# First norm, modulation rows and condition rows of a two-block fp32 layer, rearranged over the engines

## The reference

```
mx = (silu(c) @ ada_w + ada_b).reshape(6, 1024)        # 48 groups of 128 columns: j = 0..47
mc = (silu(c_ctx) @ ada_w + ada_b).reshape(6, 1024)    # only its first two rows are read
hx = x   * rsqrt(mean(x*x)   + EPS) * norm1_g * (1 + mx[1]) + mx[0]
hc = ctx * rsqrt(mean(ctx*ctx) + EPS) * norm1_g * (1 + mc[1]) + mc[0]
ux, uc = hx @ w_in, hc @ w_in
# gates f = lb + (1-lb)*sigmoid(u_f) ; k = 1-f ; q = silu(u_q) ; bidirectional scan over the tokens
# mx[2] scales the mixer's residual, mx[3], mx[4] modulate the second norm, mx[5] the FFN's residual
```

## Time and profile before

| what | value |
|---|---|
| median of 3 runs | 951.21 us (949.1 to 951.27) |
| the profiled execution's own time | 950.52 us |
| its span in the trace | 948.3 us |
| TensorE matmuls busy | 874.2 us (92%) |
| VectorE busy | 588.7 us (62%) |
| ScalarE busy | 463.9 us (49%) |
| GpSimd busy | 409.7 us (43%) |
| mean granted clock of TensorE | 0.965 |

### The profile page before, as it was taken

How to read it: one execution, slowest core, us unless ns; L and a number is a source line. 1 busy time by engine, 2 the same in 40 slices (tenths; PEclk the granted TensorE clock), 3 DMA queues, 4 the chain that set the end, 5 groups by cost and what they waited for, 6 DMA issues and landing times. The chain is left out here.

```text
span 948.3 us, 16413 instructions
## 1 busy us (share of the span) xinstructions
PE 874.2 (92%) x6668; PEld 832.1 (88%) x6668; DVE 588.7 (62%) x1218; ACT 463.9 (49%) x755; POOL 409.7 (43%) x180
## 2 busy tenths in 40 slices
PE   3599978999997899999999989999999999999995
PEld 0268968999976899999999989989999999999995
DVE  4888856555457878777667567977545543333335
ACT  3363223333274566555555576445444565455543
POOL 3455412221010028888888710000000788888881
PEclk9779997999999899999999999999999999999997
DMA  9677653443156645656665544625444455566641
GB/s 354 248 246 255 234 200 113 132 134 101 54 184 216 184 152 175 207 181 182 191 180 179 179 143 138 197 67 177 135 134 134 154 180 184 177 185 189 182 152 46
DMA packets 46043, 162.53 MB, mean 171 GB/s; under 512 B 5248, under 2 KB 5392, under 8 KB 45840
## 3 DMA queue, kind: packets, MB, share of 16 engines
q1 hardware_dynamic: 45680, 160.43, 52.6%
q10 hardware_dynamic: 288, 1.05, 0.4%
HBM read 160.41 MB, written 1.05 MB: 170 GB/s over the span
## 5 line engine op out<-in xcount | busy, mean ns | idle before, releaser
L476 POOL TENSOR_TENSOR wlo<-raw,whi 128x1024 fp32r<-128x1024 f32 x160 | 387.5, 2441 | 461.8 <-ACT whi L1069 461.7
L1069 ACT ACTIVATE whi<-raw 128x1024 fp32r<-128x1024 f32 (+1 forms) x253 | 258.1, 1026 | 85.6 <-PE bank L604 44.5
L604 PE MATMUL bank<-h2l,whi 128*128 128x256 f32 x848 | 240.4, 284 | 2.5 <-DVE h2l L1459 2.4
L600 PE MATMUL bank<-h2h,whi 128*128 128x256 f32 x848 | 241.6, 285 | 0.5 <-ACT h2h L1286 0.5
L602 PE MATMUL bank<-h2h,wlo 128*128 128x256 f32 x848 | 239.9, 283 | 0.0
L1459 DVE SCALAR_TENSOR_TENSOR accs<-bank,vec,accs 128x189 f32<-128x189 f32 (+4 forms) x440 | 161.2, 433 | 72.2 <-ACT accs L1331 72.2
L604 PEld LDWEIGHTS bank<-h2l,whi 128*128 128x128 f32 x848 | 162.7, 192 | 3.5 <-DVE h2l L1459 3.5
L600 PEld LDWEIGHTS bank<-h2h,whi 128*128 128x128 f32 x848 | 162.7, 192 | 1.4 <-ACT h2h L1286 0.7
L602 PEld LDWEIGHTS bank<-h2h,wlo 128*128 128x128 f32 x848 | 162.7, 192 | 0.1
L476 DVE TENSOR_TENSOR wlo<-raw,whi 128x1024 fp32r<-128x1024 f32 (+1 forms) x93 | 104.5, 1131 | 40.6 <-ACT whi L1069 40.2
L886 PE MATMUL bank<-gl,whi 128*128 128x256 f32 x352 | 99.7, 283 | 1.3 <-DVE gl L1456 1.3
(11 more groups left out here) (303 smaller groups left out, 1673.5 us busy)
## 6 DMA issues: line engine op xcount, KB each, us to landing
raw<-in_up SPq DMA_DIRECT2D x88, 512.0 KB, 3.6
raw<-in_w_in SPq DMA_DIRECT2D x45, 512.0 KB, 3.7
raw<-in_down SPq DMA_DIRECT2D x44, 512.0 KB, 3.9
ada_buf<-in_adaT SPq DMA_DIRECT2D x40, 512.0 KB, 4.3
raw<-in_w_out SPq DMA_DIRECT2D x16, 512.0 KB, 3.6
raw<-in_w_in_t SPq DMA_DIRECT2D x12, 512.0 KB, 4.7
ada_sc<-in_ada SPq DMA_DIRECT2D x8, 512.0 KB, 14.0
raw<-in_wk SPq DMA_DIRECT2D x8, 512.0 KB, 3.8
```

The lines of the kernel that those rows point to most:

```text
L476: return e.tensor_tensor(wlo[:, j % HL, 0:k], raw[:, j % RAW, 0:k], whi[:, j % HL, 0:k].bitcast(F32), ALU.subtract)
L600: e.matmul(ps, wh[:, k, :], xh(k), start=k == 0, stop=False)
L604: t = e.matmul(ps, wh[:, k, :], xl(k), start=False, stop=k == KTILES[name] - 1)
L1069: e.activation(whi[:, j % HL, 0:(k1 - k0) * 128], raw[:, j % RAW, 0:(k1 - k0) * 128], ACT.Copy).then_inc(S.hi.up(j))
```

## The change

Seven things are changed, all before the end of the scan:

- The condition rows come as two DMAs of 4 KB into one partition (`crow`), get one silu, and TensorE spreads them over 128 partitions into four PSUM banks (`row_of`). The 16 sums of groups 0 to 7 read them there. ScalarE copies the x row to `cb` in an SBUF place that lasts, so that the later reload and silu are gone.
- The squares go into 8 tiles of their own (`sqs`), and TensorE sums all of them, 32 small matmuls into one bank, ahead of the scale rows. GpSimd's additions are gone.
- The norm's row is copied to SBUF (`rsx`), and GpSimd multiplies x and context with it (`xr`). VectorE then needs one `tensor_scalar` (times amul, plus shift) for each half tile, written to a PSUM bank; ScalarE's addition of the shift is gone.
- `amul` is made ahead of the last pair of sums, and columns 0 and 1 are made side by side by `lins`.
- The loads are put in another order: a short first part of `vec` and all of x and context first, the convolution's vectors later, the chunks 16 to 18 before the wait for the first low halves.
- The groups 16 to 47 go round three buffers of their own (in the places of `kT` and `vM`, which are written later).
- Their sums stand elsewhere: one behind each ff column in place of two, none in front of `qx` in place of eight, and two in each of the eight calls of `beside`, which had none. The last eight stay where they were.

```diff
-ADA_OF = [[j] + ([j + 6] if j < 2 else []) + (list(range(12 + j, 48, 2)) if j > 3 else []) for j in range(6)]
+ADA_OF = [[j] + ([j + 6] if j < 2 else []) for j in range(6)] + [list(range(16 + j, 48, 3)) for j in range(3)]
...
+        put("sqs", 94 + 16, [128, 8, 512])
+        put("crow", 94, [1, 2, 1024])
+        put("xr", 94, [128, 8, 512])
+        put("rsx", 92, [128, 512])
+        put("ada_kT", 20, [128, 2, 1024])
+        put("cb", 28, [128, 1024])
+        put("ada_vM", 32, [128, 1024])
...
+        def ada_at(j):
+
+            s = next(s for s in range(9) if j in ADA_OF[s])
+            if s < 6:
+                return s, M["ada_buf"][:, s, :]
+            return s, M["ada_kT"][:, s - 6, :] if s < 8 else M["ada_vM"][:, :]
+
+        def ht_bank(k):
+            return aux_bank(("ht", k))
+
+        def row_of(who):
+
+            first = 4 if who else 2
+            return psum[:, first:first + 2, :].rearrange("p a b -> p (a b)")
...
+            one_row = cst[0:1, 1:2].broadcast_to((1, 128))
...
+            for who, ring, first in ((0, lin_ring, 0), (1, aux_ring, 4)):
+                w.wait_ge(S.const, "cst")
+                w.wait_ge(S.rowc, "crow")
+                for half in range(2):
+                    slot, _ = ring.take(("row", who, half), S.ada, 7)
+                    t = e.matmul(banks[first + slot], one_row, M["crow"][:, who, half * 512:half * 512 + 512], start=True,
+                                 stop=True)
+                t.then_inc(S.rows.up(("cb", "cbx")[who]))
+
+            slot, _ = aux_ring.take("x", S.by_row, "x")
+            w.wait_ge(S.const, "ones")
+            for i in range(8):
+                w.wait_ge(S.sqx, i)
+                for b in range(4):
+                    t = e.matmul(banks[4 + slot][:, b:b + 1], M["sqs"][:, i, b * 128:b * 128 + 128], ones[:, 0:1],
+                                 start=i == 0 and b == 0, stop=i == 7, skip_group_check=True)
+            t.then_inc(S.total.up("x"))
+            w.wait_ge(S.ident, 0)
+            spread("x", aux_bank("x"))
...
             for k in range(KT):
-                if k == 4:
-                    means("x", M["ssx"], 4, S.ssx, 7, (S.scaled, 7))
...
-            for j in range(8):
+            for k in range(KT):
+                ht_bank_free[k] = aux_ring.take(("ht", k), S.hcl, k)[1]
+
+            columns = []
+            for j in range(2):
+                slot, free = lin_ring.take(("ff", j), S.sgf, j)
+                columns.append(("w_in", IN_FF + j, banks[slot][:, :], free))
+            lins(columns, hc_all)
+            for j in range(2, 8):
...
+            w.wait_ge(S.crow, "ctx")
+            e.activation(crow[:, :, :], crow[:, :, :], ACT.Silu).then_inc(S.rowc.up("crow"))
...
-            w.wait_ge(S.cb, "first")
-            e.activation(cb[:, :], cb[:, :], ACT.Silu).then_inc(S.rowc.up("cb"))
-            w.wait_ge(S.cbx, 0)
-            e.activation(cbx[:, :], cbx[:, :], ACT.Silu).then_inc(S.rowc.up("cbx"))
+            w.wait_ge(S.rows, "cb")
+            e.activation(M["cb"][:, :], row_of(0), ACT.Copy).then_inc(S.rowc.up("cb"))
             for i in range(8):
                 w.wait_ge(S.x[i // 4], 0)
+                e.activation(M["sqs"][:, i, 0:L], xT[:, i, :], ACT.Square)
                 w.wait_ge(S.ctx[i // 4], 0)
-                out = M["ssx"]
-                if i:
-                    w.wait_ge(*sq_free["x", i])
-                    out = sq_at(("x", i))
-                e.activation(out[:, 0:L], xT[:, i, :], ACT.Square)
-                e.activation(out[:, L:2 * L], M["ctxT"][:, i, :], ACT.Square).then_inc(S.sqx.up(i))
+                e.activation(M["sqs"][:, i, L:2 * L], M["ctxT"][:, i, :], ACT.Square).then_inc(S.sqx.up(i))
             w.wait_ge(S.const, "cst")
             sqrt_next()
             w.wait_ge(S.total, "x")
             root("x", aux_bank("x")[:, 0:4])
+            by_row("x", M["rsx"][:, :], aux_bank("x"))
...
-            splits(HL)
-            w.wait_ge(S.mod, "shift")
+            splits(2)
             for k in range(KT):
-                ht = hs_at(k)
                 w.wait_ge(S.scaled, k)
-                for v in range(2):
-                    t = e.activation(ht[:, v * L:v * L + L], ht[:, v * L:v * L + L], ACT.Identity,
-                                     bias=M["mod"][:, k, v:v + 1])
-                t.then_inc(S.hch.up(("shift", k)))
-                w.wait_ge(S.hch, ("shift", k))
-                e.activation(M["hch"][:, k, :], ht, ACT.Copy).then_inc(S.hch.up(("hi", k)))
+                e.activation(M["hch"][:, k, :], ht_bank(k), ACT.Copy).then_inc(S.hch.up(k))
+                if k in (3, 6):
+                    splits(2 + k // 3)
...
             for j in range(KT):
-                w.wait_ge(S.rowc, "cbx")
+                w.wait_ge(S.rows, "cbx")
+                w.wait_ge(S.rowc, "cb")
                 if j:
                     w.wait_ge(own_dve, own_dve.n)
-                ada_sum(j, 1, junk[:, :], cbx[:, :]).then_inc(own())
+                ada_sum(j, 1, junk[:, :], row_of(1)).then_inc(own())
                 w.wait_ge(own_dve, own_dve.n)
-                ada_sum(j, 0, ada_buf[:, slot_of(j), :], cb[:, :]).then_inc(S.ada.up(j))
-                if j == 4:
+                ada_sum(j, 0, None, row_of(0)).then_inc(S.ada.up(j))
+                if j == 1:
                     inverse("x")
-            w.wait_ge(S.rows, "turned")
-            two = (128, 8, 2)
-            tt(mod[:, 8:16, :], aux_bank("turned")[:, 0:16].rearrange("p (j w) -> p j w", w=2),
-               col("ada_b", 8, 8).unsqueeze(2).broadcast_to(two), ALU.add).then_inc(S.mod.up("scale"))
-            w.wait_ge(S.mod, "scale")
-            stt(amul[:, :, :], mod[:, 8:16, :], 1.0, col("norm1_g", 0, 8).unsqueeze(2).broadcast_to(two), ALU.add,
-                ALU.mult).then_inc(S.mod.up("amul"))
+                if j == 6:
+                    w.wait_ge(S.rows, "turned")
+                    tt(mod[:, 8:16, :], aux_bank("turned")[:, 0:16].rearrange("p (j w) -> p j w", w=2),
+                       col("ada_b", 8, 8).unsqueeze(2).broadcast_to(two), ALU.add).then_inc(S.mod.up("scale"))
...
-            w.wait_ge(S.spread, "x")
-            w.wait_ge(S.mod, "amul")
-            for k in range(KT + 3):
+            w.wait_ge(S.mod, "shift")
+            for k in range(KT + 2):
                 if k < KT:
-                    if k >= 4:
-                        w.wait_ge(S.hcl, k - 4)
-                    for v, src in enumerate((xT, M["ctxT"])):
-                        t = stt(hs_at(k)[:, v * L:v * L + L], src[:, k, :], amul[:, k, v:v + 1],
-                                aux_bank("x")[:, v * L:v * L + L], ALU.mult, ALU.mult)
+                    w.wait_ge(*ht_bank_free[k])
+                    w.wait_ge(S.xr, k)
+                    for v in range(2):
+                        t = e.tensor_scalar(ht_bank(k)[:, v * L:v * L + L], M["xr"][:, k, v * L:v * L + L],
+                                            amul[:, k, v:v + 1], mod[:, k, v:v + 1], ALU.mult, ALU.add)
                     t.then_inc(S.scaled.up(k))
-                if k >= 3:
-                    i = k - 3
-                    w.wait_ge(S.hch, ("hi", i))
-                    tt(M["hcl"][:, i, :], hs_at(i), M["hch"][:, i, :].bitcast(F32), ALU.subtract).then_inc(S.hcl.up(i))
+                if k >= 2:
+                    w.wait_ge(S.hch, k - 2)
+                    tt(M["hcl"][:, k - 2, :], ht_bank(k - 2), M["hch"][:, k - 2, :].bitcast(F32),
+                       ALU.subtract).then_inc(S.hcl.up(k - 2))
...
                 ada_step()
-                ada_step()
...
-            for _ in range(8):
-                ada_step()
...
             for h in range(4):
                 los(ch("w_in", IN_Q + h) + HL)
                 w.wait_ge(S.sg, ("q", h))
-                w.wait_ge(S.ada, 39)
...
                     if kind == "g":
                         gate_value(n)
+                ada_step()
+                ada_step()
...
-            ssx = M["ssx"][:, :]
-            for i in range(1, 8):
-                w.wait_ge(S.sqx, i)
-                if i > 1:
-                    w.wait_ge(S.ssx, i - 1)
-                e.tensor_tensor(ssx, ssx, sq_at(("x", i)), ALU.add).then_inc(S.ssx.up(i))
+            w.wait_ge(S.by_row, "x")
+            for k in range(KT):
+                for v, src in enumerate((xT, M["ctxT"])):
+                    t = e.tensor_tensor(M["xr"][:, k, v * L:v * L + L], src[:, k, :], M["rsx"][:, v * L:v * L + L],
+                                        ALU.mult)
+                t.then_inc(S.xr.up(k))
...
-            e.dma_start(vec[:, :], D["vec"]).then_inc(S.vec.up(0), 16)
+            e.dma_start(vec[:, 0:NVEC1], D["vec"][:, 0:NVEC1]).then_inc(S.vec.up(0), 16)
+            tokens(0)
+            tokens(1)
+            e.dma_start(ident[:, :], D["ident"]).then_inc(S.ident.up(0), 16)
             scale(0)
-            for j in range(6):
+            for j in range(7):
                 scale(j + 1)
```

(25 more changed lines are left out.)

90 lines of the change are left out of this document (38 added, 52 removed).

## The result

The changed kernel takes 938.97 us (median of 4 runs, 938.22 to 939.7) against 950.69 for the kernel before on the same chip (949.1 to 951.27): ratio 0.9879 [0.9862, 0.9896]. It is faster, by about half of what was forecast (23.5 us), and it ends 1 us above the forecast's range. The profiled execution took 938.86 with a span of 937.1.

The account below looks back on a forecast made before the run. TensorE was taken as the bound, standing still ahead of the scan's end only in the opening and behind q. Gains of 10.1 and 13.4 us make 23.5: 951.21 - 23.5 = 927.7 us, range 920 to 938.

Parts of the forecast that it names:

- Behind q: Between the last q column and `S0`: without the eight sums, 6.2 us in place of 19.6, gain 13.4 us.
- The sums in the scan: Sixteen sums moved into eight scan levels, hidden in VectorE's idle 4.63 us: price 0; uncovered 19.6 us, chance 0.07.
- The opening: From the start to the second column's end, 56.2 us in place of 66.3: gain 10.1 us.
- sums with a bank operand: VectorE's 16 opening sums, one input in a bank, priced at 1.2 us each while GpSimd works.
- scale products: TensorE's 16 scale matmuls in the opening, 32 records at 0.44 us: 14.1 us, ending at 36.5.
- first product to the end of the pass: Two columns side by side, 48 matmuls, 12 at the low level in 5.7 us and 36 in 7.9, ending at 56.2.
- The 32 matmuls of 128x1: TensorE's sum of squares in the opening, 64 records at 1.90 us for 16: 7.6 us, ending at 20.6.
- `crow`: TensorE's first four matmuls, spreading the condition rows, 8 records of 512 columns: 4.98 us, ending at 13.0.
- The shift's addition: VectorE's addition of the shift after the last two sums in the opening: 0.2 us.
- Root and spread: Root, reciprocal and the spread's four matmuls with handovers, before the scale matmuls: 1.8 us, an estimate, ending at 22.4.
- pair and copy: Last steps before the first product: first half-tile pair on VectorE 0.8 us, ScalarE's copy from a bank 0.6.
- third rival: TensorE at 1.2 GHz from first matmul to the pass's end: +9.4, +14.1, +7.0, 30.5 us, so 958.2; chance 0.03.

Follow-up runs that it names:

- experiment 1: The kernel before with its own opening, plus only the change's loads, buffers, lasting `cb` and moved sums: 936.78 us.
- experiment 8: Changed kernel, VectorE's last two sums and shift addition moved before the transposes' wait, squares summed by 8 matmuls of 512 columns, no spread: 929.59 us.
- experiment 4: Changed kernel with four dense f32 matmuls of 512 columns, result unused, ahead of `crow`'s: 933.37 us.
- Experiment 3: Changed kernel with GpSimd adding the eight squared tiles, and 4 matmuls of one column on TensorE in place of 32: 935.41 us.
- Experiment 9: Changed kernel with the eight bias columns first copied to a PSUM bank, from which the shift's addition reads them: 935.38 us.
- experiment 10: Changed kernel with the first two columns of w_in one after the other instead of side by side: 941.12 us.
- experiments 5 and 6: 5: changed kernel, VectorE's last sums and shift addition before the transposes' wait, 933.46 us; 6: that with Experiment 3 and four scale-product steps before the sum, 928.56 us.
- experiments 2: Changed kernel with the sums of groups 16 to 47 back at their old places, in their own buffers: 952.1 us.

## Why the prediction was half right

**Behind q: right.** Forecast 13.4, measured 13.1. `S0` follows with 0.94 us of idle, at the full clock (3.81 us with the tail, forecast 3.5).

**The sums in the scan: right.** Priced 0; experiment 1 has them and keeps the whole gain. From 160 to 240 us TensorE is busy 79.13 of 80.

**The opening: forecast 10.1, measured -0.6.** The structure was right, a chain of TensorE's work with VectorE's pieces behind it, and these terms hold: sums with a bank operand beside GpSimd 1.22 us (1.2; one with both operands in SBUF took 1.23, so the fixed cost that the Trainium skill gives for a PSUM source, "VectorE: DVE Perf Modes", the TRN2 errata, did not show), x products 0.72 to 0.75 (0.73), scale products 14.36 (14.1), first product to the end of the pass, when ScalarE reads its bank at 66.67, 13.4 (13.6), from there to q's end 67.2 (67.0). The terms that fail account for the first product at 53.23 instead of 42.6:

- "The 32 matmuls of 128x1 are 64 records at 1.90 us for 16: 7.6." They took 13.81, **6.2 us** more. This is the step that failed. The row was read at 258.89, where TensorE had come from nearly 100 us of work at a granted clock of 1.00; here it came from rest and from `crow`'s records at half pace. In this place the one-column records didn't come up to the full pace, and dense ones did (experiment 8); brought to it, they didn't keep it (experiment 4). The right price stood in the trace of the kernel before, in the opening itself, for the same instruction (first row below): 0.23 us for each record, at a granted clock of 0.50; 64 of them would be 14.7. Experiment 3 took 56 of the 64 away, and the first product came 2.8 us earlier; more of the 6.2 wasn't to be had that way, since the chain then waits for GpSimd's additions, to 22.6.
- `crow`: 4.98 forecast from a row that was partly at the full pace, 7.16 measured at half: 2.2.
- The shift's addition: 0.2 forecast, 2.15 measured: 1.95. I had asked of the sums and of the half tiles whether GpSimd holds them, and not of this. In the kernel before it took 0.17 us at 43.11, when GpSimd's low halves had only just begun (43.09; second row below). Experiment 9 shows the hold, by what frees it.
- Root and spread 2.6 instead of 1.8; pair and copy 1.8 instead of 1.4: 1.2. Against it, TensorE started at 6.71, not 8.0: 1.3.

The two rows of the kernel before:

```profile
30.30 1.84 PE L661 MATMUL bank<-ones,ssx 128*128 128x1 f32 x8 [10.09 <-POOL ssx L2072]
...
43.11 0.17 DVE L1456 TENSOR_TENSOR mod<-mod,vec 128x16 f32<-128x16 f32 x1
```

Together 6.2 + 2.2 + 1.95 + 1.2 - 1.3 = 10.3 of the 10.6 us. My third rival had the mechanism, half pace from the first matmul, with +9.4 for the records ahead of the scale products (by its own rows 9.7: 7.6 more for the sum, 2.1 for `crow`; measured 8.4), but tied it to the scale products and the pass as well. I argued against it with four records that were quick after a short pause; those were dense, and so were the scale products, which were quick here too. The rival should have been split at that point, and its first third given a chance of its own.

**From the chain to the end.** The first score is 12.6 us earlier than before, the span is 11.2 shorter. The missing 1.4 lies behind the scan, where TensorE's waits are for the same tiles in both kernels. Up to one of these waits (2.37 us for `sq`, over at 623.72 before and at 611.09 now) the lead is still 12.6 us; at the next, for `h2h` (661.83 and 650.79), it is 11.0. The windows of 16.3 us that follow the first wait, before and now:

```profile
623.72:640.00 16.28, 16.28 (x125) 16.28 (x126) 14.05 (x27) 6.40 (x13) 0.00 (x0) 0.90 0.21 68
```

```profile
611.09:627.40 16.31, 16.31 (x112) 16.31 (x113) 12.93 (x26) 6.07 (x12) 0.00 (x0) 0.79 0.22 68
```

TensorE is busy all the time in both, at a mean granted clock of 0.90 and of 0.79, with 13 records fewer now. So the 1.6 us go where the same work stood longer at the lower level; the change touches nothing there, and why it stood longer in this execution is open.

**The change's own trade.** Taking the sum off GpSimd cost 14 us on the engine that the chain runs through, and GpSimd's next work, the products of x, had to wait for that very sum. VectorE's sums didn't need it either: in experiment 3 they took 1.22 us beside GpSimd's additions, since their row stands in a bank. Of the changes in the opening the pass of two columns pays (experiment 10), the bank operands let the sums run at 1.22 us (no experiment takes them out, so what they are worth in the run is not shown), and the sum on TensorE costs 3.6 us of the run (experiment 3).

## What to carry to other kernels

Take the price of a record from a row that stands behind the same kind of work: the row behind the scan gave 0.12 us, the one in the opening 0.23, and the opening was what was priced. Ask for each group of matmuls whether it is dense or one column wide: in this opening dense records came up to the full pace (experiment 8), while one-column records didn't in 13.8 us and lost it where they had it (experiment 4), and `crow`'s 512 columns with a single row of weights stayed at half pace for all of their 7.16 us. Where two engines share a stretch, look for tiny instructions with both operands in SBUF on VectorE: their cost is whatever is left of GpSimd's stream, and moving them earlier can make it longer; an operand in a bank frees them. Work that is moved off a slower engine is paid for on the engine that it goes to; put it there only where that engine has a hole in time, as TensorE had from 14 to 23 us for the scale products once GpSimd summed.

## What was not expected of the hardware

- The granted clock is shown as 1.00 from 6 to 28 us in the changed kernel, but its records run at the same pace as those of experiment 4 under a shown 0.50 (64 in 13.81; 52 in 11.3), and in experiment 3 the eight of 0.234 us each stand in a window shown as 1.00 too. Early in an execution the pace had to be read from the durations.
- A VectorE addition of 16 columns took 0.17, 0.42, 2.15, 3.75, 4.13 and 6.15 us, by what GpSimd was doing; the long ones whose rows are shown here beside GpSimd's, in the changed kernel and experiments 5 and 6, end within 0.04 us of the end of GpSimd's last product. It can slip in between two products (0.42) or miss several such gaps.
- The same scale products behind the same records took from 14.36 to 15.94 us over the changed kernel and experiments 2, 5, 9 and 10, and behind one and the same wait the granted clock was 0.90 in one profile and 0.79 in another: two profiles of the same work can differ in how long TensorE stays at the lower level.
- A reciprocal over 128x512 took 3.35 us on VectorE, 0.18 over 128x4.
